# Tiles of 32 rows in the expert stages of a two-layer trunk, with the turns done by VectorE in blocks

## The reference

```
scores = sigmoid(h @ router_w)                       # (tokens, 16)
# best group of 4 experts, best two in it, gates = their scores, normalised
for e in range(16):
    a = silu(h @ w_gate[e]) * (h @ w_up[e])          # 1024 -> 512
    out = out + gates[:, e:e+1] * (a @ w_down[e])    # 512 -> 1024
x = x + g2 * out
```

## Time and profile before

| | us |
|---|---|
| median of three runs | 1119.46 |
| lowest and highest | 1117.81, 1120.41 |
| profiled execution | 1120.89 |
| its span, first to last instruction | 1119.3 |
| TensorE busy | 969.8 (87%) |
| VectorE, ScalarE, GpSimd busy | 308.2, 226.0, 102.5 |

### The profile page before, as it was taken

How to read it: one execution, slowest core, us unless ns; L and a number is a source line. 1 busy time by engine, 2 the same in 40 slices (tenths; PEclk the granted TensorE clock), 3 DMA queues, 4 the chain that set the end, 5 groups by cost and what they waited for, 6 DMA issues and landing times.

```text
span 1119.3 us, 16030 instructions
## 1 busy us (share of the span) xinstructions
PE 969.8 (87%) x5879; PEld 575.6 (51%) x5880; DVE 308.2 (28%) x695; ACT 226.0 (20%) x432; POOL 102.5 (9%) x174
## 2 busy tenths in 40 slices
PE   3799999999986999999999929999959988877980
PEld 2247434566446555555555516877445544544540
DVE  1104101864253111111111145357241111111113
ACT  2210102343020122122222223034021211111211
POOL 2000101004202200000000130000010000000002
PEclk9899999999995999999999969999959999999995
DMA  9977778549949698799999954646178999999973
GB/s 343 353 284 277 283 268 360 213 166 336 242 160 355 218 384 325 301 395 385 395 375 388 387 196 142 225 197 236 76 259 313 365 387 402 397 392 404 391 271 112
DMA packets 90564, 334.64 MB, mean 299 GB/s; under 512 B 9312, under 2 KB 23280, under 8 KB 74000
## 3 DMA queue, kind: packets, MB, share of 16 engines
q1 hardware_dynamic: 74112, 289.77, 67.9%
q0 software_dynamic: 10016, 33.89, 10.1%
q10 hardware_dynamic: 6400, 10.49, 2.7%
HBM read 307.84 MB, written 28.74 MB: 301 GB/s over the span
## 4 chain that ended last, share of the span: by engine, by line
PE 45%; DMA 18%; DVE 4%; issue 1%; ACT 1%; POOL 0%; ACTq 0%; SPq 0%; POOLq 0%; DVEq 0%
PE bank L1216 18%; DMA weight_ring<-in_w_up_dram 9%; PE bank L1234 9%; DMA weight_ring<-in_w_gate_dram 8%; PE bank L1014 3%; PE bank L1130 2%; PE bank L1017 2%; PE bank L1200 2%; PE bank L1261 2%; PE bank L1225 1%; PE bank L1092 1%; PE bank L1065 1%; DMA weight_ring<-y_by_expert,slot_numbers 1%; PE bank L1077 1%; PE bank L970 0%
## 5 line engine op out<-in xcount | busy, mean ns | idle before, releaser
L1216 PE MATMUL bank<-weight_ring,qk_tokens 128*64 128x256 f32 x2560 | 304.9, 391 | 32.6 <-DMA weight_ring<-in_w_up_dram 29.6
L1216 PEld LDWEIGHTS bank<-weight_ring,qk_tokens 128*64 128x64 f32 x2560 | 193.1, 141 | 139.8 <-issue 64.6
L1234 PE MATMUL bank<-weight_ring,qk_tokens 128*64 128x512 f32 x640 | 152.9, 598 | 0.0
L1622 DVE TENSOR_TENSOR qk_tokens<-qk_tokens,bank 64x256 f32<-64x256 f32 x80 | 33.8, 423 | 328.7 <-ACT qk_tokens L904 328.7
L1014 PE MATMUL bank<-weight_ring 128*128 128x256 f32 (+1 forms) x320 | 97.8, 464 | 4.9 <-ACT weight_ring L795 3.1
L1017 PE MATMUL bank<-weight_ring 128*128 128x512 f32 (+1 forms) x256 | 84.9, 489 | 0.0
L1130 PE MATMUL bank<-weight_ring 128*128 128x512 f32 x192 | 83.4, 594 | 1.4 <-ACT weight_ring L864 1.4
L1014 PEld LDWEIGHTS bank<-weight_ring 128*128 128x128 f32 x320 | 61.8, 196 | 40.3 <-issue 34.8
L904 ACT ACTIVATE qk_tokens<-bank 64x256 f32<-64x256 f32 x80 | 30.1, 376 | 206.2 <-PE bank L1216 205.9
L1234 PEld LDWEIGHTS bank<-weight_ring,qk_tokens 128*64 128x64 f32 x640 | 42.4, 136 | 54.2 <-issue 45.7
L904 ACT ACT_TABLE_LOAD x40 | 51.3, 1283 | 85.1 <-issue 74.9
(11 more groups left out here) (173 smaller groups left out, 731.4 us busy)
## 6 DMA issues: line engine op xcount, KB each, us to landing
weight_ring<-in_w_gate_dram SPq DMA_DIRECT2D x64, 1024.0 KB, 9.0
weight_ring<-in_w_up_dram SPq DMA_DIRECT2D x64, 1024.0 KB, 8.9
weight_ring<-in_w_down_dram SPq DMA_DIRECT2D x64, 1024.0 KB, 9.5
weight_ring<-in_w_mod_dram SPq DMA_DIRECT2D x24, 2048.0 KB, 8.1
weight_ring<-in_w_in_dram SPq DMA_DIRECT2D x12, 1024.0 KB, 10.0
qk_tokens<-h_by_expert POOLq DMA_DIRECT2D x40, 256.0 KB, 7.2
y_by_expert<-qk_tokens ACTq DMA_DIRECT2D x80, 128.0 KB, 7.0
weight_ring<-in_w_out_dram SPq DMA_DIRECT2D x4, 2048.0 KB, 11.7
```

The lines of the kernel that those rows point to most:

```text
L1216: mm = pe.matmul(pb[hf][64 * r:64 * r + 64, 0:256], hTe[:, k, :], w[:, k, hf * 256:(hf + 1) * 256], start=(k == 0), stop=(k == KD - 1), ti ...
L1234: mm = pe.matmul(pb[4][64 * r:64 * r + 64, :], aTe[:, k, :], wdown(n)[:, k, r * 512:(r + 1) * 512], start=(k == 0), stop=(k == KF - 1), ti ...
L1622: V.tensor_tensor(ae[:, hf * 256:(hf + 1) * 256], sg[:, hf * 256:(hf + 1) * 256], pb[hf][SLOTS:P, 0:256], ALU.mult).then_inc(s_a[l], 1)
```

## The change

Tiles get 32 rows. The edits that belong to it:

- PE's products have four stationary operands of 32 columns side by side: two column halves of gate and two of up (one bank, 256 columns each), and four quarters of w_down's 1024 columns.
- The turns of rows and activations go to VectorE, which transposes blocks of 32x32. So that these blocks fall where the products need them, the model dimension is dealt to partitions in another way, and with it the rows of w_gate, w_up and w_down in the loads: w_down is now read as `(g c k) n -> c g k n` with c = 2. A tile's rows are loaded as four quarters of 256 columns to 128 partitions, `s (q n) -> q s n`, and y is stored in the same way in one copy.
- There are two row buffers and two output buffers; the loops of GpSimd, ScalarE and VectorE take two tiles per pass, and the number of tiles is rounded up to an even one.
- The rows of the first four tiles (not one) are picked from the tokens.
- In layer 0 each expert has at least two tiles, and PE does the gate and up products of a tile before the w_down products of the one before. In layer 1 an expert has at least one tile, and w_down follows its own gate and up.
- The table of rows has 68 tiles of 32 (it had 32 of 64). The zero rows are written by 17 copies of 128 rows and, for the output table, 9 more, in place of 32 copies of 64 rows and up to 16 copies between the tables.

```diff
-SLOTS = 64
+SLOTS = 32
...
-    NTILE = 2 * NALL * P // SLOTS + NE
+    NTILE = 2 * NALL * P // SLOTS + 2 * NE + 4
+    AHEAD = P // SLOTS
+    Q = D // AHEAD
...
+    LEAST = [2 if n == NALL else 1 for n in NT]
...
                 for (w, d, k), hf in ((gate, 0), (up, 0), (gate, 1), (up, 1), (down, 0), (down, 1)):
-                    rows_ = slice(hf * k // 2 * P, (hf + 1) * k // 2 * P)
-                    order = "(k p) n -> p k n" if k == KF else "(p k) n -> p k n"
-                    src = (w[l, e, rows_, :].rearrange(order, p=P) if isinstance(e, int)
-                           else w[l, bass.ds(e, 1), rows_, :].rearrange("a " + order.replace("-> p k", "-> p (a k)"), p=P))
+                    part = slice(hf * k // 2, (hf + 1) * k // 2)
+                    if k == KD:
+                        src = (w[l, e].rearrange("(p k) n -> p k n", p=P)[:, part, :] if isinstance(e, int)
+                               else w[l, bass.ds(e, 1)].rearrange("a (p k) n -> p a k n", p=P)[:, 0, part, :])
+                    else:
+                        src = (w[l, e].rearrange("(g c k) n -> c g k n", c=2, k=k)[:, :, part, :] if isinstance(e, int)
+                               else w[l, bass.ds(e, 1)].rearrange("a (g c k) n -> a c g k n", c=2, k=k)[0, :, :, part, :])
                     yield d[:, hf * k // 2:(hf + 1) * k // 2, :], src
...
-                with pool.Fori(1, total) as T:
-                    pool.wait_ge(s_hTp[l], T + 1)
-                    pool.dma_start(hrow, hsort[bass.ds((T + 1) * SLOTS, SLOTS), :]).then_inc(s_hrow[l], 16)
+                with pool.Fori(0, pairs) as n:
+                    for i in range(2):
+                        pool.wait_ge(s_hT[l], n * 2 + (3 + i))
+                        pool.dma_start(hrow[i], hsort[bass.ds((n * 2 + (AHEAD + i)) * SLOTS, SLOTS), :].rearrange("s (q n) -> q s n", q=AHEAD)
+                                       ).then_inc(s_hrow[i][l], 16)
...
-                    nc.scalar.copy(ysb, pb[4][:, :]).then_inc(s_y[l], 1)
+                    nc.scalar.copy(ysb[i], pb[4][:, 0:Q]).then_inc(s_y[l], 1)
                     act.wait_ge(s_y[l], T + 2)
-                    for hf in range(2):
-                        act.dma_start(ysort[bass.ds(T * SLOTS, SLOTS), hf * 512:(hf + 1) * 512],
-                                      ysb[hf * SLOTS:(hf + 1) * SLOTS, :]).then_inc(s_yd[l], 16)
+                    tile_rows = slice(T * SLOTS, (T + 1) * SLOTS) if isinstance(T, int) else bass.ds(T * SLOTS, SLOTS)
+                    act.dma_start(ysort[tile_rows, :].rearrange("s (q n) -> q s n", q=AHEAD), ysb[i]).then_inc(s_yd[i][l], 16)
...
+                        for g in range(4):
+                            w, f = (wgate(n), wup(n))[g // 2], (g % 2) * Q
+                            mm = pe.matmul(pb[0][32 * g:32 * g + 32, 0:Q], hTe[:, k * SLOTS:(k + 1) * SLOTS],
+                                           w[:, k, f:f + Q], start=(k == 0), stop=(k == KD - 1), tile_position=(0, 32 * g))
+                    mm.then_inc(s_gu[l], 1)
...
+                        for g in range(4):
+                            mm = pe.matmul(pb[4][32 * g:32 * g + 32, 0:Q], aTe[:, k * SLOTS:(k + 1) * SLOTS],
+                                           wdown(n)[:, k, g * Q:(g + 1) * Q], start=(k == 0), stop=(k == KF - 1), tile_position=(0, 32 * g))
                     mm.then_inc(s_d[l], 1)
...
+                def turn_rows(i, loaded):
+
+                    dve.wait_ge(s_hrow[i][l], loaded * 16)
+                    V.transpose(hTe.rearrange("p (b s) -> p b s", b=KD), in_blocks(hrow[i], KD)).then_inc(s_hT[l], 1)
```

More of the change, by code:

```diff
@@ L182, in hybrid_trunk @@
         wtk = sb("gate_weights", [P, 2, NALL])
[L183 removed]
+        tab = [mrow[0:1, 32 * l:32 * l + 32].bitcast(I32) for l in range(DEPTH)]
         def slot(n, a=0, m=SLOT):
@@ L380, in hybrid_trunk @@
         s_y = lsem('s_y')
-        s_yd = lsem('s_ystored')
+        s_yd = [lsem(f's_ystored_{i}') for i in range(2)]
         s_g2 = Stage(sem("s_g2"), 32)
@@ L1251, in expert @@
-                def expert(e, use, n):
-                    lo = pe.value_load(tab[l][0:1, bass.ds(e, 1)], min_val=0, max_val=NTILE)
-                    hi = pe.value_load(tab[l][0:1, bass.ds(e + 1, 1)], min_val=0, max_val=NTILE)
-                    with pe.Fori(lo, hi) as T:
-                        tile(T, n, use)
-                pe.wait_ge(s_pick.sem, s_pick.at(l, 1))
-                for k in range(KD):
-                    for t in range(NT[l]):
-                        mm = pe.matmul(pb[5][:, k * SLOTS:(k + 1) * SLOTS], model_rows(h2[:, t, :], k), picked[:, t, :],
-                                       start=(t == 0), stop=(t == NT[l] - 1))
@@ L1263, in _, with arrived, gate_up @@
-                mm.then_inc(s_hTp[l], 1)
-                pe.wait_ge(s_pos.sem, s_pos.at(l, 1))
-                with pe.Fori(0, (NE - 1) // RING) as i:
-                    for j in range(RING):
-                        expert(i * RING + j, i + 1, l + j)
-                expert(NE - 1, (NE - 1) // RING + 1, NE - 1 + l)
+                def arrived(n, part, use):
+                    pe.wait_ge(s_we[n % RING][part], use * 16 + weights_at(l, n % RING, 0))
+                def gate_up(T, n, use, first):
+                    pe.wait_ge(s_hT[l], T + 1)
+                    if LEAST[l] == 2 and not isinstance(T, int):
+                        pe.wait_ge(s_a[l], T)
+                    for k in range(KD):
+                        if first and k % HK == 0:
+                            arrived(n, 2 * (k // HK), use)
+                            arrived(n, 2 * (k // HK) + 1, use)
+                        for g in range(4):
[3 more added lines that the diff above has]
+                    mm.then_inc(s_gu[l], 1)
@@ new lines, in later_tiles, with first_tile_index @@
+                def later_tiles(lo, hi, n, use):
+                    with pe.Fori(lo + 1, hi) as T:
+                        gate_up(T, n, use, False)
+                        down(T - 1, n, use, True)
+                def first_tile_index(e):
+                    return pe.value_load(tab[l][0:1, e:e + 1], min_val=1, max_val=NTILE - 8)
+                pe.wait_ge(s_tab.sem, s_tab.at(l, 1))
+                hi = first_tile_index(1)
+                for t in range(NT[l]):
+                    pe.wait_ge(s_pick.sem, s_pick.at(l, t + 1))
+                    for hf in range(2):
+                        mm = pe.matmul(pb[6 + hf][:, :], picked[:, t, :], h2[:, t, hf * MH:(hf + 1) * MH], start=(t == 0), stop=(t == NT[l] - 1))
@@ new lines, in _ @@
+                dve.wait_ge(s_tot.sem, s_tot.at(l, 1))
+                pairs = dve.value_load(tab[l][0:1, NE + 1:NE + 2], min_val=LEAST[l] * NE // 2 - 2, max_val=NTILE // 2 - 4)
+                with dve.Fori(0, pairs) as n:
+                    for i in range(2):
+                        dve.wait_ge(s_gu[l], n * 2 + (4 + i))
+                        turn_rows(i, n + 1)
+                        product(n * 2 + (3 + i))
+                        dve.wait_ge(s_d[l], n * 2 + (3 + i))
+                        turn_a()
```

238 lines of the change are left out of this document (125 added, 113 removed).

## The result

The kernel after takes 2245.4 us (median; 2241.2 to 2249.2 in four runs), the kernel before 1118.9 us beside it: a ratio of 2.007, with an interval of 2.002 to 2.011. Half of the speed is gone. The forecast was 2180 us, its own range 2030 to 2330.

A forecast was written before the change was run, and what follows sets the result against it. w_down's copies, held to two DMA engines, were taken to bound both expert stages: 13 x 56.8 us to 1192 in layer 0, 13 x 53.4 to 2144 in layer 1, plus a 32.3 us tail: 2180 us, own range 2030 to 2330.

The forecast's parts named there:

- The bottleneck and what decides: Expert stages: PE races a stream of 6.29 MB of weights per expert; the change's effect on the stream decides.
- Engines by the outermost dimension: Copies: engines are the largest number up to 16 dividing both outermost sizes; w_down two, rows and y four; unequal sides open.
- Rate of one engine: DMA engines: 26.6 KB/us each, no faster alone; one w_down copy 19.7 us on two engines, a pair 39.4.
- The period: Expert stages, busiest engine per expert: 39.4 + 9.9 plus 3.0 us per tile, 56.8 us in layer 0, 53.4 in layer 1.
- PE's product with w_mod: Front of layer 0: w_mod's load waits behind the first w_down, landing at 232.4, 24 us late.
- Layer 0's end: Layer 0's expert stage: 448 + 13 x 56.8, plus 5, ends at 1192 against 647, costing 545 us more.
- Layer 1's end: Layer 1's expert stage: from 1445, 13 x 53.4 gives 2139, plus 5 for the last tile: 2144.
- PE's tile: Expert products on PE: 64 + 32 instructions at 54 to 60 ns, 5.2 to 5.8 us per tile of 32 rows.
- PE or VectorE is the bound: Rival, expert stages: four operands of 32 don't overlap at 256 columns; about 1200 us if copies are even; chance 0.015.
- only the rows and y stay on four engines: Rival, copies: w_down is spread, busiest engine 22.3 us per expert in layer 0, 19.0 in layer 1; 1150 us; chance 0.025.
- even: Rival, copies: all dealt over 16 engines after all; -79 us, 1040 us, range 1030 to 1065; chance 0.12.
- The point from which it decides: w_down's engine count: between 8 and 16; with 8, 21.7 us per expert is above the 17.5 of now.

The follow-up runs named there:

- kernel 11: The kernel before with only w_down read as (g c k), c=2 outermost, and gate and up columns in matching order: 2233.2 us, ratio 1.994 to before.
- kernel 3: The kernel after with w_down read with an outermost dimension of 4 in place of 2, columns matched: 1706.7 us, ratio 1.524 to the kernel before.
- kernel 4: The kernel after with w_down read with an outermost dimension of 8 in place of 2, columns matched: 1546.1 us, ratio 1.380 to the kernel before.
- kernel 2: The kernel after with w_down rows placed so its source is 128 outermost, gate and up columns matched: 1167.4 us, 1.041 to the kernel before.
- kernel 5: The kernel after with the rows' load and y store each in four copies of 32 partitions, w_down unchanged: 2199.7 us, 1.965 to the kernel before.
- kernel 10: The kernel after with layer 1's small loads issued behind layer 0's expert loop, not ahead of expert 3's load: 2243.5 us, 2.004 to the kernel before.
- kernel 6: The kernel after with w_down 128 outermost and the rows' load and y store each in four copies: 1080.9 us, ratio 0.965 to the kernel before.
- kernel 8: The kernel after with w_down in an outermost dimension of 8 and rows and y in four copies each: 1436.7 us, from one run.
- kernel 9: The kernel after with each w_down copy cut in two of 64 partitions, rows and y in four copies: 1238.5 us, 1.106 to the kernel before.

## Why the prediction was right

The mechanism was right: w_down on two engines, and an expert's period set by their work. That the period came out so near (0.1 us off in layer 0, 1.1 in layer 1) was partly luck, for two of its terms were off against each other. Step by step, in its order:

- *The bottleneck and what decides.* "What the change does to the stream decides": right. PE busy 42% instead of 87%, and kernel 11 shows the stream alone doubling the time.
- *Engines by the outermost dimension.* The open step, a copy with unequal sides. Settled: 2, 4, 8 and 16 engines by the small packets of kernels 3, 4 and 2, and 0.13 of the DMA in the stretch where the pair is alone. The 62 stores of y leave 8184 packets, 62 x (128 + 4): four engines each. For the load of rows the same count doesn't show four (kernel 5), and its four engines stay an assumption. The Trainium skill (DMA: Bandwidth & Descriptors, section Why a DMA increments its semaphore by 16 and not by 1) gives the same rule, and here it holds for 2, 4 and 8 against 128.
- *Rate of one engine.* 26.6 forecast, 26.5 measured for two alone. With all queues at work it is lower: 25.0 in the period of kernel 5, if the engine never stood empty, and 20.4 to 21.7 in the mean over all busy engines of a stretch.
- *The period.* 56.8 and 53.4 forecast, 56.7 and 54.5 measured, but by terms that don't hold. Rows and y in one copy each cost 0.9 us per tile more than spread, and not the 2.25 between 3.0 and 0.75 (kernel 5), 3.4 us too much in layer 0; the weights' part is 52.5 and not 49.3, 3.2 us too little. The sum was better than its terms.
- *PE's product with w_mod* at 232.4 forecast, 236.5 measured, from 208.2.
- *Layer 0's end* 1192 forecast, 1223.7 measured. All 32 us lie ahead of expert 3 (kernel 10), where the two-copy window and the gate copies that share a pair's engines were not in the sum. Layer 1 has the same fault once more: expert 0 goes out at 1300.7 (1269 + 32), and expert 3's w_down at 1495, where the forecast had expert 2's through at 1445 (1445, 32 and 18 make 1495).
- *Layer 1's end* 2144 forecast, 2214 measured: 32 carried over, 18 at its front, 15 in 13 periods, and the last product and its tile took 10 and not 5. The tail took 27 us and not 32.
- *PE's tile* of 5.2 to 5.8 us: hidden here, and seen in kernel 2 where nothing holds it up, 3.45 + 1.73 us and 0.0 to 0.1 between. So *PE or VectorE is the bound* was rightly left with little: a turn of 128x256 takes 0.65 us on VectorE (first row, of the kernel after), and four operands of 32 overlap at 256 columns (54 ns per instruction).

```profile
L1640 DVE STREAM_TRANSPOSE qk_tokens<-qk_tokens 128x256 f32<-128x256 f32 x54 | 34.8, 645 | 866.2 <-PE bank L1225 852.3
...
665.15 3.45 PE bank L1221 x64
668.60 1.73 PE bank L1233 x32
670.33 3.45 PE bank L1221 x64
```

Of the rivals, "only the rows and y stay on four engines" was priced at 1150 and, built as kernel 2, takes 1167; "even" was priced at 1040 and takes 1081 as kernel 6. The point from which it decides was put between 8 and 16 engines: kernel 4 at 8 is 38% slower than before, so that holds with a wide margin. The sum for it, 21.7 us per expert, was wrong: with the small copies spread as that sum has them, it forecast 1170 us and kernel 8 takes 1437.

## What to carry to other kernels

Look at the outermost dimension of both sides of every large copy after a change of layout, before anything else: 2 or 4 there leaves the other engines idle, and neither the bytes nor the addresses show it. The count of small packets per copy (on SP's and ACT's queues) and the DMA share in a stretch where it runs alone tell how many engines it had. Often the layout can be had another way: here the order in which PE reads gate and up columns gives w_down 128 rows outermost at no cost that shows, and with the small copies cut in four as well the new tiles beat the old by 3.5%.

A small copy on engines shared with large ones is priced by its landing, not by its bytes, wherever something waits for it.

## What was not expected of the hardware

- A store of 128 KB on four engines landed after 28 to 37 us beside weight copies on the same engines (kernel 4), some twenty times the 1.5 us that the sum gave for its own work on an engine; another store was in flight ahead of it.
- With w_down in copies of 512 KB to 64 partitions from rows 32 KB apart, 16 busy engines moved 293 GB/s (kernel 9), and 227 where little but w_down moved; 412 and 416 with copies to 128 partitions from rows 16 KB apart (kernel 6). Which difference does it is open.
- The rate of a busy engine is not one number. In layer 1 it was 21.7 KB/us in the mean with w_down on two engines, 19.7 on four (kernel 3), 16.1 on eight (kernel 4) and 25.2 on sixteen with all copies spread (kernel 6: 412 / (16 x 1.02)); two alone moved 26.5.
- Behind a pair of w_down copies on two engines the issue of one small copy took 19.4 us of SP's time (0.37 before), yet moving it away gained nothing.
